# Seven products for eight: the MLP's down projection by block products over pairs of output tiles

## The reference

```
def sq_relu_mlp(h, lp):
    return jnp.square(jax.nn.relu(h @ lp["w_up"])) @ lp["w_down"]
# D_MODEL = 1024, D_FF = 4096, float32
xp = xp + sq_relu_mlp(rmsnorm(xp, norm_mlp_g[l]), lp)
xs = xs + sq_relu_mlp(rmsnorm(xs, norm_mlp_g[l]), lp)
y_prompt = rmsnorm(xp, final_norm_g); y_sample = rmsnorm(xs, final_norm_g)
```

## Time and profile before

| | |
|---|---|
| median of 3 runs | 1023.48 us (1021.34 to 1028.16) |
| profiled execution | 1021.9 us, its span 1020.1 us |
| granted TensorE clock, mean | 0.998 |
| PE busy | 986.9 us (97%) |
| weight loads (PEld) busy | 892.7 us (88%) |
| DVE busy | 526.4 us (52%) |
| ACT busy | 298.1 us (29%) |
| POOL busy | 444.5 us (44%) |

### The profile page before, as it was taken

How to read it: one execution, slowest core, us unless ns; L and a number is a source line. 1 busy time by engine, 2 the same in 40 slices (tenths; PEclk the granted TensorE clock), 3 DMA queues, 4 the chain that set the end, 5 groups by cost and what they waited for, 6 DMA issues and landing times.

```text
span 1020.1 us, 19818 instructions
## 1 busy us (share of the span) xinstructions
PE 986.9 (97%) x8511; PEld 892.7 (88%) x8511; DVE 526.4 (52%) x731; ACT 298.1 (29%) x598; POOL 444.5 (44%) x284
## 2 busy tenths in 40 slices
PE   5999998998999999999999999999999999999997
PEld 5989898765677777999965899999999999999997
DVE  5789999478655555562255365421342144114443
ACT  7334275465444442220144122200120022002222
POOL 4545687500011102655220255555555555555551
PEclk9999999999999999999999999999999999999999
DMA  7323365504377763632291032322233222322222
GB/s 225 90 66 84 104 190 147 169 37 186 134 274 279 279 266 136 217 88 84 101 403 51 22 86 83 101 84 84 83 96 91 84 84 85 102 84 83 84 83 88
DMA packets 140556, 130.39 MB, mean 128 GB/s; under 512 B 13477, under 2 KB 133170, under 8 KB 136630
## 3 DMA queue, kind: packets, MB, share of 16 engines
q1 hardware_dynamic: 134888, 88.55, 28.8%
q0 software_dynamic: 2304, 37.75, 9.6%
q10 hardware_dynamic: 3278, 2.83, 0.8%
HBM read 123.53 MB, written 5.03 MB: 126 GB/s over the span
## 4 chain that ended last, share of the span: by engine, by line
PE 80%; DVE 12%; ACT 2%; DMA 2%; POOL 2%; issue 1%; SPq 1%; DVEq 0%; ACTq 0%; POOLq 0%
PE gps L587 56%; PE gps L947 5%; PE aux L961 3%; PE aux L988 3%; PE gps L1103 1%; PE gps L1185 1%; PE aux L967 1%; PE gps L1023 1%; DVE act_lo L1708 1%; PE gps L723 1%; PE aux L899 1%; PE aux L1116 1%; DMA xs<-in_x_prompt_dram 1%; POOL wlo L505 1%; PE aux L978 1%
## 5 line engine op out<-in xcount | busy, mean ns | idle before, releaser
L587 PE MATMUL gps<-act_hi,whi 128*128 128x272 f32 x912 | 265.8, 291 | 6.2 <-POOL wlo L516 3.5
L502 POOL TENSOR_SCALAR whi<-wraw 128x1024 fp32r<-128x1024 f32 (+1 forms) x109 | 115.0, 1055 | 359.5 <-PE gps L587 296.8
L587 PE MATMUL gps<-act_lo,whi 128*128 128x272 f32 x912 | 264.2, 290 | 0.0
L587 PE MATMUL gps<-act_hi,wlo 128*128 128x272 f32 x912 | 263.7, 289 | 0.0
L505 POOL TENSOR_TENSOR wlo<-wraw,whi 128x1024 fp32r<-128x1024 f32 (+1 forms) x109 | 256.4, 2352 | 9.1
L587 PE MATMUL gps<-h_hi,whi 128*128 128x272 f32 x640 | 185.7, 290 | 0.0
L587 PE MATMUL gps<-h_lo,whi 128*128 128x272 f32 x640 | 185.0, 289 | 0.0
L587 PE MATMUL gps<-h_hi,wlo 128*128 128x272 f32 x640 | 184.6, 288 | 0.0
L587 PEld LDWEIGHTS gps<-act_hi,whi 128*128 128x128 f32 x912 | 172.4, 189 | 7.2 <-issue 4.2
L587 PEld LDWEIGHTS gps<-act_hi,wlo 128*128 128x128 f32 x912 | 172.3, 189 | 0.3 <-issue 0.2
L587 PEld LDWEIGHTS gps<-act_lo,whi 128*128 128x128 f32 x912 | 172.1, 189 | 0.0
(11 more groups left out here) (374 smaller groups left out, 1529.9 us busy)
## 6 DMA issues: line engine op xcount, KB each, us to landing
wraw<-in_w_up_dram SPq DMA_DIRECT2D x32, 512.0 KB, 4.1
wraw<-in_w_down_dram SPq DMA_DIRECT2D x32, 512.0 KB, 3.7
wraw<-in_w_in_dram SPq DMA_DIRECT2D x14, 512.0 KB, 4.2
kv<-in_cache_mem_k_dram SPq DMA_DIRECT2D x7, 1024.0 KB, 6.9
kv<-in_cache_mem_v_dram SPq DMA_DIRECT2D x7, 1024.0 KB, 13.8
wraw<-in_w_mem_k_dram SPq DMA_DIRECT2D x16, 256.0 KB, 3.0
wraw<-in_w_mem_v_dram SPq DMA_DIRECT2D x16, 256.0 KB, 3.2
wraw<-in_w_out_dram SPq DMA_DIRECT2D x8, 512.0 KB, 4.8
```

Of the source, the lines that this page charges most:

```text
L502: nc.gpsimd.tensor_scalar(whi[:, slot, 0:n], wraw[:, slot, 0:n], 1.0, 1.0, ALU.mult, ALU.mult).then_inc(pool_step, 1)
L587: mm = nc.tensor.matmul(out_of(a), w_of(w, k), x_of(x, k, part), start=(k == 0 and s == 0), stop=(k == k_tiles - 1 and s == 2))
```

## The change

A group's eight down tiles become four pairs (`PAIRS`). For a pair, the weight is cut in halves of the contraction and into its two output tiles, the hidden activations in halves of the contraction and of the tokens; the four output blocks (2 output tiles x 2 token halves) come from seven products of 4 contraction blocks x 3 matmuls of 272 columns, where four blocks with two terms each took eight. Four sums of weight blocks are made on DVE (`pair_sums`). The seven weight blocks are rounded on ACT (`pair_high`), their low parts made on POOL (blocks 0, 2, 3, 6) and DVE (1, 4, 5) (`pair_low`), into one set of seven slots that is refilled for the next pair as PE frees each. Raw pair weights have buffers of their own (`praw`, two, 1 MB each). The mixes of activation blocks are made after the up tiles (`up_tile`, `mix_high`): one 272-column mix for each of tiles 0 to 3, three for each of tiles 4 to 7. Outputs gather in four banks, `aux` and `gps` in turn; ACT copies two products out before a third and a sixth are added to their banks (`pair_copy`), DVE adds and subtracts the rest into XT.

More of the change, by code:

```diff
@@ L65 @@
 NORM_BASE = [sum(k for _, k in NORMS[:i]) for i in range(len(NORMS))]
-MLP = [(_kind, _g, _j) for _g in range(GROUPS) for _kind in ("up", "down") for _j in range(8)]
-MLP_AT = {m: i for i, m in enumerate(MLP)}
+PAIRS = 4
+PRODUCTS = ("A11_B11", "S1_R1", "S3_R3", "A12_B21", "S2_R2", "S4_B22", "A22_R4")
+BANK_OF = (0, 2, 3, 0, 1, 2, 3)
+POOL_LOW = (0, 2, 3, 6)
+DVE_LOW = (1, 4, 5)
+REST_0, HALF_0, HI_0 = 128, 17, 32
 ORDER = (2, 3, 1, 0)
@@ new lines, in pair_part @@
+            def pair_part(q, i, ks):
+                g, p = divmod(q, PAIRS)
+                out = (aux, gps)[p % 2][:, BANK_OF[i], 0:HALF]
+                first_use = i in (0, 1, 2, 4)
+                for k in ks:
[12 more added lines that the diff above has]
+                            pe.wait_ge(mlp_lo, 16 * g + 8 + 2 * k + (1 if i in (3, 5) else 2))
+                    for n, (w, x) in enumerate(((0, 0), (1, 0), (0, 1))):
+                        mm = nc.tensor.matmul(out, (pw_hi, pw_lo)[w][:, i, 128 * k:128 * k + 128], moving(i, k, x),
+                                              start=(first_use and k == 0 and n == 0), stop=(k == 3 and n == 2),
+                                              skip_group_check=True)
+                if 3 in ks:
+                    mm.then_inc(pair_ps, 1)
@@ L1231, in _ @@
             pe.wait_ge(nx_var, 6)
-            pe.wait_ge(tile_free[0], (T_MLP + len(MLP)) // 2)
-            for i, z in Y_ORDER[:4]:
+            pe.wait_ge(pair_ev, 5 * 15 + 3)
+            for i, z in Y_ORDER[:3]:
                 y_turn(i, z)
-            pe.wait_ge(tile_free[1], (T_MLP + len(MLP)) // 2)
+            pe.wait_ge(nx_acc, 20)
+            for i in range(5):
+                n = 128 if i < 4 else TS
+                nc.tensor.matmul(aux[0:n, 3, i:i + 1], acc[:, 128 * i:128 * i + n], ones[:, 0:1],
+                                 start=(i == 0), stop=True, skip_group_check=True)
             pe.wait_ge(nx_sq, 5 + 8 * 3)
@@ new lines, in _ @@
+            for g in range(GROUPS):
+                for j in range(8):
+                    up_tile(8 * g + j)
+                    if j == 1:
+                        pair_sums(4 * g, 0)
+                        pair_sums(4 * g, 1)
+                    if j == 2:
+                        pair_low(4 * g, 1)
+                    if j == 3:
+                        pair_sums(4 * g, 2)
+                    if j == 5:
+                        pair_sums(4 * g, 3)
+                        pair_low(4 * g, 4)
+                    if j == 6:
+                        pair_low(4 * g, 5)
+                for p in range(PAIRS):
+                    down_pair(4 * g + p)
@@ L2169, in _ @@
+            gather_square(3, 6)
             dve.wait_ge(nx_ps, 4)
```

311 lines of the change are left out of this document (216 added, 95 removed).

## The result

The changed kernel takes **1050.3 us** (median of 4 runs, 1049.6 to 1054.3), the kernel before 1022.6 beside it: a ratio of 1.026 (95% interval 1.022 to 1.030). PE has 192 matmuls fewer and the kernel is 27.6 us slower by the medians. The profiled run took 1049.6 us with a span of 1047.7.

What follows compares the result with a forecast made beforehand. PE alone was taken to set the MLP's pace. Three groups at +7.6 us (22.7) and the last at +3.1 gave +25.8 on 1021.9, 1047.7; with the median 1.6 higher, 1049 us, 8-in-10 range 1012 to 1063.

Steps and rivals of the forecast that it cites:

- PE's saving: Down tiles of all groups: 192 fewer matmuls at 126 ns each save 24.2 us, 6.05 per group.
- The late low part at T = 2.75: DVE's last low part of pair 0 ends 2.75 us after the group's last up tile (T = 0).
- The stall: Before pair 1, groups 0 to 2: PE idles 8.7 us for load, POOL's two splits and low part; bounds 5.3 and 12.
- Pairs at DVE's pace: Pairs 1 to 3: DVE, held by POOL, needs 11.85 us against PE's 10.57; waits 2.3, 1.3, 1.3, together +4.9 per group.
- The clock: After the gap before pair 1: 1.3 us lost at reduced clock, hidden in the 2.3 us wait, so nothing added.
- The first group: Group 0: no term of its own; counted like groups 1 and 2 at +7.6 us.
- The last group: Group 3: final-norm work on ACT and DVE makes pairs wait 2.8, 3.2 and 3.2 us; -6.05 + 9.2 = +3.1.
- the tail: After the last product: changes little, nothing within 1 us.
- Rival C: Late low parts of tile 6 or 7 stop PE within pair 0: +4 to +6 us per group, 1063 to 1073; chance 0.12.
- Rival A: The hand-over stalls, but pairs keep PE's pace because DVE is held less: 1015 to 1025 us; chance 0.22.
- Rival B: Faster, the saving stays: stall before pair 1 below 4.7 us and DVE's holding cheap, 999 to 1012; chance 0.14.

Runs made afterwards that it cites:

- e4: The kernel before the change, with seven of eight contraction blocks in each down tile, that part of the product left out: 1000.5 us against 1025.1, ratio 0.977.
- e2: The changed kernel, with the next group's first two up units loaded after pair 3's weights and split by POOL after the pairs' low parts: 1030.6 us, ratio 1.0045.
- e1: The changed kernel, with SP loading the next group's first two up units ahead of pair 2's weights: 1047.6 us, ratio 1.023.
- e5: The kernel of e2, with all seven low parts of pairs 1 to 3 made on DVE: 1040.0 us, ratio 1.015.
- e9: The kernel of e5, where POOL's first split of a group waits for the last low part of the group before: 1021.7 us, ratio 0.997.
- e3: The changed kernel, where POOL writes zeros in place of its four low parts per pair, so it does not read SBUF there: 1031.2 us, ratio 1.0055.
- e10: The kernel of e9, with ACT's copy of product 1 earlier and the last group's final-norm work in its last pair: 1020.8 us, ratio 0.9947.
- e11: The kernel of e2, with ACT's copy of product 1 earlier and the last group's final-norm work in its last pair: 1023.9 us, ratio 0.999.

## Why the prediction was right

The time (1049 against 1050.3), the sign and the mechanism held: load, splits and low part follow each other and stop PE before pair 1, and a DVE held by POOL makes the pairs late. That the total agrees to 1 us is luck, since terms missed by up to 10 us and cancelled. Groups 0 to 2 together, in us, against the kernel before:

| Term | in the sum | measured |
|---|---|---|
| PE's saving | -18.2 | -18.2 (by e4) |
| gap before pair 1 | +26.1 | +19.4 |
| waits in pairs 1 to 3 | +14.7 | +4.6 |
| waits in the up tiles and pair 0 | 0 | +5.6 |
| half clock | 0 | +7.9 |
| in no wait of the profile | 0 | +2.7 |
| together | +22.7 | +22.0 |

The single steps, by what they measured:

- **PE's saving, -24.2.** e4: -24.6, and -24.1 by the MLP parts. Right.
- **The late low part at T = 2.75.** In the second group it ended at 778.83, T = 2.4. Right.
- **The stall, 8.7 per group.** 5.7, 6.6 and 7.1: oversized by 2 us. The term by its parts in the second group: POOL began at T = 9.45 instead of 10.3, the splits took 7.1 instead of 7.5, pair 1 began at 18.0 instead of 19.3 (the parts of my sum make 19.1), and pair 0 itself ended 0.8 later, for the wait of 0.7 for the copy of product 1, which I had not in the sum. The load was faster than I took it. The DMA's rate in 0.4 us slices of 778 to 794 us, whose first transfer starts at 779.6:

```profile
GB/s 0 0 0 0 3 90 166 306 348 348 343 348 348 346 344 348 348 319 292 288 293 289 76 0 0 0 0 0 0 0 0 0 0 0 0 0 0 0 0 0
```

  With several loads queued it is 348 GB/s, not the 290 that I took from the earlier trace rows; it falls to 290 once the last one is left. The third load landed 7.0 us after the first was issued: 3 x 524 KB at 348 GB/s are 4.5, and 2.5 fixed. The page "DMA: Bandwidth & Descriptors" of the Trainium skill has a fit of 2.0 us plus bytes over 436 GB/s, made for loads issued from GpSimd; an estimate by it is 5.6 us for the same. The 7.0 us of these loads, issued by SyncE, do not agree with it. The 348 GB/s do agree with the limit of about 358 GB/s per core that the same page names in the section "Where 436 GB/s comes from".
- **Pairs at DVE's pace, 11.85, +4.9 per group.** The period was 11.52 (800.87 to 812.39 to 823.92, the last low part that DVE makes in each pair). The waits were 0.4, 0.7 and 0.7, 1.9 in all: oversized by 3 us. The half clock is the smaller part of it: in a middle group of e2, which lost nothing to the clock, the same three waits are 0.9, 0.7 and 0.7. Pair 1's was 0.9 there where I had 2.3, and those of pairs 2 and 3 are 0.7 for 1.3. In the third group, after 6 us at half clock, only pair 3's is left.
- **The clock, "hides in the 2.3 us wait".** It did not hide. It cost 3.2, 1.6 and 3.1 us in groups 0 to 2, 7.9 together and more than the waits that it was to hide in. Waits of pairs 1 to 3 and clock together are 3.4 us in the second group, against 4.9.
- **The first group.** Nothing in the sum, and some 4.5 us in the table over the others. DVE starts late there, behind the reciprocal of the norm, and catches up beside POOL's splits: PE waits 1.1 and 0.8 for DVE in the up tiles and 2.3 in pair 0, and behind that last wait another 1.6 us went to half clock.
- **The last group, +3.1, and the tail, 0.** Together 4.5. The waits were 0.9, 3.0 and 1.5 instead of 9.2 in all, and 0.7 in pair 0; the half clock behind the wait of 3.0 took 1.7, and the tail grew by 3. DVE's timeline of the end:

```profile
1032.54 0.44 DVE L2422 TENSOR_TENSOR XT<-gps,XT 128x272 f32<-128x272 f32 x1
1033.81 0.73 DVE L2253 TENSOR_TENSOR acc<-acc,sqb 128x544 f32<-128x544 f32 x1 [0.83 <-ACT sqb L1407]
1037.13 0.16 DVE L2447 TENSOR_SCALAR rsx<-aux 128x4 f32<-128x4 f32 x1 [2.60 <-PE aux L1349]
```

  From the last eviction to the end of the span it is 15.2 us, against 12.1 before. A pair finishes *two* tiles at its end, so a tile more of squares and sums (one step of DVE's `acc`, and the ten small matmuls that wait for it) stands behind the last product. This is half of the growth: from the eviction to `rsx` it is 4.6 us, against 2.9 before (1008.02 to 1010.96). The other 1.4 lie behind `rsx`, where PE's transposes of the output ran at a granted clock of 0.57 (1036.3 to 1040.3); with nothing lost to the clock the tail is 14.1, 13.8 and 13.7 in e1, e5 and e9. I had counted an eviction for an eviction and not asked how much of the final work the form leaves for afterwards.
- **Rival C** did not happen in the changed kernel; e1 showed it, with 3.7 to 5.5 us of waits for `rx_lo` in the middle of pair 0. **Rival A** is about what e3 shows from the other side: without the holding the pairs keep PE's pace. That it still took 1031 is 17.7 us of gaps, 8.4 of half clock in groups 0 to 2, 3.4 of waits in the first group and 2.0 in the tail. **Rival B** needed the stall below 4.7 us *and* pairs at PE's pace; e9 and e10 reach its sign by taking away both. Two of the rivals' bounds are 1 to 2 us off what their own terms give (B's 1012 is 1013.5 from the median, C's 1063 to 1073 is 1065 to 1071).

What stays open: 1.1 us of a group in e2 (94.8, of which 90.7 is matmuls and 3.0 waits) belong to no wait in the profile; 0.6 of it is left in e10. The first group's delay was read from the trace and not tested. Why the clock stayed at half for 6 us in the third group and for less than 4 in the second is open too.

## What to carry to other kernels

Fewer matmuls pay only if what feeds them keeps up: count the work that moves to VectorE and GpSimd, and lay it out in the order of each queue, since here 24 us of TensorE's time were bought with 51 us elsewhere, of which other orders and another share of the low parts gave back 33 (e10). Where GpSimd reads SBUF beside VectorE, ask *when* it runs before asking how much: keeping its splits to a stretch where VectorE has slack was worth 16 us by itself (e9), and a wait added to an idle engine can make a kernel faster. A tuned wait shows its successor at once (the copy, then the eviction), so read the next limit before pricing the removal of the first. And price the half clock behind every gap of a few us as a term of its own: here it was 11 us in all, as much as the waits for the copy.

## What the runs showed of the hardware

- GpSimd writing zeros does not hold VectorE (e3: 0.69 for a sum of 512 columns beside it); GpSimd subtracting does (1.4 to 1.6), and a split of 1024 columns adds up to 2.2 us (e9: 2.62 where 0.44 is the price).
- TensorE's granted clock was 0.50 in the first 2 us after a gap of 6.6 us, 0.71 in the next 2 and 1.00 after that; after one of 7.1 us it was 0.50 for 6 us. The same wait of 2.29 us in pair 0 of the first group was followed by half clock in the changed kernel and in e2 (1.6 and 1.7 us lost) and by full clock in e11. A middle group of e10, with one gap of 0.7 us, takes 0.6 us more than its matmuls and that wait.
- Loads of 512 KB in 512-byte pieces moved 348 GB/s while two or more were under way, and 290 when one was left.
